# A fixed first expert with its rows gathered turned, two weight pieces loaded earlier, and the gather moved inside an expert block

## The reference, cut to what matters

```
h = layer_norm(ALPHA * x + mix, ln1_g, ln1_b)
logits = h @ router_w + router_b          # top 4 of 32 experts
gates = softmax(top_v)
# tokens sorted by expert into blocks; for each block b with expert e:
gu = xb @ w_gu[e] + b_gu[e]               # 1024 x 2048
act = (clip(up) + 1) * min(gate, 7) * sigmoid(1.702 * min(gate, 7))
out = act @ w_down[e] + b_down[e]         # 1024 x 1024
y = layer_norm(ALPHA * h + sum_k gate_k * out_k, ln2_g, ln2_b)
```

## Time and profile before

| | |
|---|---|
| median of 3 runs | 1522.77 us (1522.66 to 1524.72) |
| profiled execution, its own time | 1524.9 us |
| its span | 1523.1 us |
| PE busy | 1461.6 us (96%) |
| DVE busy | 519.6 us (34%) |
| ACT busy | 263.8 us (17%) |
| POOL busy | 114.1 us (7%) |
| DMA | 507.80 MB, mean 333 GB/s |
| chain that ended last | PE 61%, DMA 25%, DVE 3% |

### The profile page before, as it was taken

How to read it: one execution, slowest core, us unless ns; L and a number is a source line. 1 busy time by engine, 2 the same in 40 slices (tenths; PEclk the granted TensorE clock), 3 DMA queues, 4 the chain that set the end, 5 groups by cost and what they waited for, 6 DMA issues and landing times.

```text
span 1523.1 us, 23088 instructions
## 1 busy us (share of the span) xinstructions
PE 1461.6 (96%) x9245; PEld 743.2 (49%) x9245; DVE 519.6 (34%) x980; ACT 263.8 (17%) x604; POOL 114.1 (7%) x100
## 2 busy tenths in 40 slices
PE   9999999999999998999999999999999999999896
PEld 7777776556777764333333333333333333333332
DVE  3652788767410156122122212211212112122123
ACT  1224214631210014100101001001001001100102
POOL 1002241010503402000000000000000000000000
PEclk9999999999999999999999999999999999999998
DMA  6346687556269648999999999999999999999995
GB/s 211 111 168 179 209 271 232 175 167 195 89 216 331 247 164 316 428 426 429 426 427 428 429 427 429 429 428 428 428 430 428 428 428 429 430 427 428 429 429 205
DMA packets 110621, 507.80 MB, mean 333 GB/s; under 512 B 12600, under 2 KB 49056, under 8 KB 85888
## 3 DMA queue, kind: packets, MB, share of 16 engines
q1 hardware_dynamic: 103884, 499.63, 82.0%
q10 hardware_dynamic: 6676, 7.29, 1.6%
HBM read 491.18 MB, written 15.72 MB: 333 GB/s over the span
## 4 chain that ended last, share of the span: by engine, by line
PE 61%; DMA 25%; DVE 3%; ACT 1%; issue 1%; DVEq 0%; SPq 0%; ACTq 0%
DMA wGU<-in_w_gu 24%; PE ps L2394 12%; PE ps L2399 11%; PE ps L1898 10%; PE ps L2381 5%; PE ps L2202 3%; PE ps L1912 3%; PE ps L2308 2%; PE ps L2216 2%; PE ps L2229 2%; PE ps L2342 2%; PE ps L2316 1%; DMA ringS<-in_ssd_proj 1%; ACT xs L1267 1%; PE ps L2329 1%
## 5 line engine op out<-in xcount | busy, mean ns | idle before, releaser
L2394 PE MATMUL ps<-wGU,xe 128*64 128x512 f32 x1536 | 342.4, 594 | 18.5 <-DMA wGU<-in_w_gu 17.8
L2399 PE MATMUL ps<-wD,aT 128*64 128x512 f32 x1024 | 226.8, 595 | 0.0
L2394 PEld LDWEIGHTS ps<-wGU,xe 128*64 128x64 f32 x1536 | 107.8, 137 | 234.5 <-issue 197.8
L1898 PE MATMUL ps<-xT,ring 128*128 128x288 f32 (+1 forms) x864 | 179.8, 409 | 1.2 <-PEq L200 0.7
L1898 PEld LDWEIGHTS ps<-xT,ring 128*128 128x128 f32 (+1 forms) x864 | 125.1, 170 | 46.0 <-issue 3.5
L2399 PEld LDWEIGHTS ps<-wD,aT 128*64 128x64 f32 x1024 | 70.7, 137 | 131.8 <-issue 127.9
L2381 PE MATMUL ps<-wGU,xe 128*64 128x512 f32 x512 | 121.3, 594 | 11.9 <-DMA wGU<-in_w_gu 11.9
L1791 DVE TENSOR_SCALAR sg<-sg 128x512 f32<-128x512 f32 x32 | 13.7, 427 | 335.4 <-ACT sg L1262 335.4
L1798 DVE COPY ysb<-ps 64x512 f32<-64x512 f32 x32 | 22.2, 694 | 304.8 <-PE ps L2403 304.8
L1262 ACT ACTIVATE sg<-ps 128x512 f32<-128x512 f32 x32 | 19.1, 598 | 471.1 <-PE ps L2386 471.1
L402 PE MATMUL ps<-xT,ring 128*128 128x288 f32 x320 | 78.1, 407 | 0.0
(11 more groups left out here) (476 smaller groups left out, 1445.1 us busy)
## 6 DMA issues: line engine op xcount, KB each, us to landing
wGU<-in_w_gu SPq DMA_DIRECT2D x128, 2048.0 KB, 37.0
wD<-in_w_down SPq DMA_DIRECT2D x64, 2048.0 KB, 37.0
ring<-in_w_in SPq DMA_DIRECT2D x21, 2048.0 KB, 9.2
out<-hst SPq DMA_DIRECT2D x8, 1024.0 KB, 6.0
ringS<-in_ssd_proj SPq DMA_DIRECT2D x4, 2048.0 KB, 10.1
wbuf<-prompt_A_rows ACTq DMA_DIRECT2D x16, 384.0 KB, 4.0
out<-Sb SPq DMA_DIRECT2D x2, 2048.0 KB
ring<-in_hg_proj SPq DMA_DIRECT2D x2, 2048.0 KB, 7.8
```

The lines of the kernel that those rows point to most:

```text
L1898: last = m.matmul(ps[h, b, 0:T], ring[c % 2][:, k, n * P + h.start:n * P + h.stop], xT[:, k, :], start=(k == 0), stop=(k == KD - 1))
L2394: last = m.matmul(ps[half[h], bank, :], xe[:, f, hx, :], wgu[n][:, k, col + CW * h:col + CW * h + CW], start=(i == 0 and k == 0), stop=False)
L2399: last = m.matmul(ps[half[h], B_Y, :], aT[:, k, i - 4, :], wdn[n][:, k, CW * h:CW * h + CW], start=(i == 4 and k == 0), stop=False)
```

## The change

1. Rows are normalised without gamma and beta, by ScalarE in place (`normal`, one activation a tile), and no longer on VectorE. Gamma and beta are applied to the turned rows: `weighed` multiplies and adds per partition from `lnT2`, which two small transposes of `lng4` fill. The copy to `xe` becomes eight small activations a block. ALPHA times gamma and beta (`w5`, `yb`) give the residual (`residual`), which VectorE makes in blocks 0 and 1.
2. The first block is always expert 0: `nb5[:, 0, 0]` is set to 1, and its tokens are found from the counts of expert 0 alone (`first_tokens`). Its rows are gathered turned, in fp32, straight from the rows (`first_rows`), in four quarters, so that `turn_x` and two copies fall away for it. Block 1 is gathered in fp32 from the rows (`gather_rows`). The bf16 parts for the loop are made in block 1 by VectorE and GpSimd (`parts`, t_hp).
3. mT lies in gA and not in gB, so that piece 5 of expert 0 is issued once the branches are merged; piece 3 of expert 1 (buffer 9) is issued after the first half of w_out. If the list is wrong, only expert 1's four pieces are loaded again.
4. In `run` the gather stands ahead of piece 2 (in block 0 ahead of `turn_g`, as before), the bias matmuls stand ahead of piece 3's, and VectorE waits for U by m_f.
5. 8 warming matmuls instead of 12 at the start; the loads of the second LayerNorm's parameters no longer wait for the last gather.

```diff
-                for _ in range(12):
+                for _ in range(8):
...
-        mT = gB
+        mT = gA
...
+                    if n == 0:
+                        sp.wait_ge(t_b3, 1)
+                        piece(1, 3, 9, m_w[9])
                 piece(0, 4, 4, m_w[4])
+                sp.wait_ge(g_m, KD)
+                piece(0, 5, 5, m_w[5])
                 sp.wait_ge(g_mx, 5)
                 piece(1, 0, 6, m_w[6])
                 sp.wait_ge(g_mx, 6)
-                piece(0, 5, 5, m_w[5])
                 piece(1, 1, 7, m_w[7])
                 sp.wait_ge(t_lg, 3)
-                sp.wait_ge(t_h, 5)
+                sp.wait_ge(t_w, 2)
                 piece(1, 2, 8, m_w[8])
-                sp.wait_ge(t_c, 10)
-                piece(1, 3, 9, m_w[9])
...
-                sp.wait_ge(m_x, end + 2)
                 sp.dma_start(lnw2[:], row(ln2_g[0])).then_inc(g_ln, 16)
...
+                def normal(j, t):
+                    rows = TILES[t][1]
+                    act.wait_ge(ln_r, 2 * j + 2)
+                    act.wait_ge(t_ht, (2, 4, 6)[j])
+                    outs = (slice(0, P),) if rows == P else (bands[2], bands[1], bands[0])
+                    for pr in outs:
+                        last = a.activation(xres[pr, t, :], xres[0:rows, t, :], ACT.Identity, scale=var[0:rows, t:t + 1], bias=nmr[0:rows, t:t + 1])
+                    last.then_inc(t_h, 1)
+                def weighed(src, f, h, i):
+                    return a.activation(xe[:, f, h, :], src, ACT.Identity, scale=lnT2[:, f % 2, 2 * h + i:2 * h + i + 1],
+                                        bias=lnT2[:, f % 2, 4 + 2 * h + i:5 + 2 * h + i])
...
+                def first_tokens(t):
+                    rows, (bank, c) = TILES[t][1], ((3, 0), (7, 32), (6, E_))[t]
+                    dstep(v.tensor_tensor(dsel[0:rows, t:t + 1], ps[0:rows, bank, c:c + 1], msk[0:rows, t, 0:1], ALU.mult))
+                    v.tensor_tensor(psel[0:rows, t, :], jcol1[0:rows, :], dsel[0:rows, t:t + 1].broadcast_to([rows, BLK]), ALU.is_equal).then_inc(m_p, 1)
...
+                def first_rows(t, quarters):
+                    rows = TILES[t][1]
+                    for j in quarters:
+                        h, i, bank = QUARTERS[j]
+                        c = CW * h + 256 * i
+                        z = xres[0:rows, t, c:c + 256].rearrange("q (p k) -> q k p", k=2)
+                        for k in range(2):
+                            last = m.matmul(ps[:, bank, BLK * k:BLK * k + BLK], z[:, k, :], psel[0:rows, t, :], start=(t == 2 and k == 0), stop=(t == 1 and k == 1))
+                        if t == 1:
+                            last.then_inc(m_x, 1)
...
+                        if i == gather_at:
+                            pe.wait_ge(m_p, b + 4)
+                            gather()
+                        if i == 3:
+                            pe.wait_ge(m_g, b * 2 + 2)
+                            for bank, col in ((B_G, 0), (B_U, D)):
+                                for h in range(2):
+                                    m.matmul(ps[half[h], bank, :], esel[:], bg3[:, col + CW * h:col + CW * h + CW], start=False, stop=False)
                         if i == 4:
-                            pe.wait_ge(m_p, b + 2)
-                            pe.wait_ge(m_xs, b + 1)
-                            for t in (2, 0, 1):
-                                gather(t)
...
+                                if head and i == 0 and k == 0:
+                                    pe.wait_ge(t_eb, 1)
+                                    m.matmul(ps[0:1, B_S, 0:64], ebc[0:64, 0:1], ident[0:64, 0:64], start=True, stop=True).then_inc(t_tb, 1)
...
+                run(0, 0, 0, None, head=True, gather=gather_rows, gather_at=4)
                 pe.wait_ge(m_ok, 1)
-                run(0, 0, 0, None)
-                run(1, 0, 6, None, (6, 7, 8, 9, 0, 1))
+                run(1, 0, 6, None, (6, 7, 8, 9, 0, 1), gather=gather_rows)
```

More of the change, by code:

```diff
@@ L1228, in _ @@
[L1228 to L1237 removed]
+                turned(3)
+                normal(1, 0)
@@ L1249, in _ @@
[L1249 to L1252 removed]
+                normal(2, 1)
+                act.wait_ge(g_mx, 6)
+                a.activation(yb[:], lnb[:], ACT.Copy, scale=ALPHA).then_inc(t_w, 1)
+                for j, (h, i, bank) in enumerate(QUARTERS):
+                    if j == 0:
+                        continue
+                    act.wait_ge(m_x, j + 1)
+                    for k in range(2):
+                        last = weighed(ps[:, bank, BLK * k:BLK * k + BLK], 2 * i + k, h, i)
+                    last.then_inc(t_xa if j < 3 else m_xc, 1)
@@ L2349, in scatter, with run @@
                         (prompt(j, B_S + j % 3) if j < 4 else samples(B_S + j % 3)).then_inc(m_s, 1)
-                def run(b, turn0, first, pair, places=None):
-                    pe.wait_ge(m_xc, b + 1)
+                def run(b, turn0, first, pair, places=None, head=False, gather=gather_parts, gather_at=2):
+                    if not head:
+                        pe.wait_ge(m_xc, b + 1)
                     for i in range(6):
+                        if head and i < 4:
+                            pe.wait_ge(*((t_x0, 1), (t_xa, 1), (t_xa, 2), (m_xc, 1))[i])
                         n, loaded = (first + i) % RING, turn0 * 64 + 16 * ((first + i) // RING + 1)
```

344 lines of the change are left out of this document (172 added, 172 removed).

## The result

The change makes the kernel slower: 1539.95 us (median of 6 runs, 1535.58 to 1547.54) against 1524.20 for the kernel before beside it (median of 6, 1522.66 to 1529.62). The ratio is 1.0107, with a 95% interval of 1.0083 to 1.0131. The forecast was 1513.9 with a range up to 1520.0, so it was wrong in sign. The experiments ran on several chips; where two of them are compared, the ratio to the kernel before, measured beside each, is the safer number. One execution of all, of a12_g4_pool, took 2172.63 us at a mean granted clock of 0.652, and its ratio leaves that one out.

A forecast was written before the change was run, and what follows sets the result against it. The stream of expert weights was taken as the bound: -8.3 (earlier 11th landing) - 1.1 (tail) + 0.5 (stream pauses) = -8.9 us, off the 1522.77 median, gives 1513.9, range 1510.5 to 1520.

The forecast's parts named there:

- a gap of about 1 us ahead of turn_a in each block: Expert loop: a sign that the forecast is right, TensorE waiting about 1 us before turn_a in every block.
- The pair of blocks: Expert loop: a block without scatter costs 0.86 more, 26.05 us; block pairs take 56.5 us until TensorE meets the stream.
- no DMA waits at all in the last blocks: End of the loop: a sign that the forecast is wrong, meaning TensorE is the bound.
- the first rival: Head: the clock stays at its upper level, so 11.4 us off, 1511.4; chance 0.2.
- The second rival: Loop: TensorE partly becomes the bound, a block costing 1.05 to 1.35 more, 1514 to 1523; chance 0.19.
- the third: Loop: slower, the uncovered activation chain costs over 1.35 more a block; at 1.6 it gives 1530; chance 0.08.
- TensorE has 5.6 us to spare: Whole loop: TensorE's blocks end at 1491.6 against 1497.2 set by the stream, 0.19 us spare a block.
- 8 warming matmuls instead of 12 end 1.7 us earlier: Kernel start: the weights are awaited there anyway, so fewer warming matmuls change the time by 0.
- Eight turning gathers in fp32: Head, behind the last choice: gathers sized by eight router matmuls of like shape, 1.08 us, 0.4 more at low clock.
- The clock: Head: the granted clock falls as before, at half until about 596, so block 0 starts at 591.3.
- Everything that brings this 11th landing forward moves the end one for one: Stream start: the first reload lands at 605.3 instead of 613.6, taking 8.3 us off the end.
- The parts beside each other: Block 1: bf16 parts take near 15 us on GpSimd and about 6 on VectorE, any wait within TensorE's slack.

The follow-up runs named there:

- a12_g4_pool: a12_g4 with the first row tile's three parts made on GpSimd behind its own two tiles instead of on VectorE: 1525.07 us, ratio 1.0011.
- a12_g4_wide: a12_g4_pool with eight more bf16 matmuls of 512 columns between the head's narrow fp32 matmuls: 1527.21 us, ratio 1.0022.
- pool_head: a12_g4_pool with 16 of the 24 fp32 records behind the last choice left out, so block 0 computes wrong rows: 1522.11 us, ratio 0.9988.
- a12_g4: The changed kernel with 12 warming matmuls and the gather ahead of turn_g (piece 4) in every block: 1525.72 us, ratio 1.0008.
- after_gather4: The changed kernel with only the gather moved back ahead of turn_g (piece 4) in every block: 1537.0 us, ratio 1.0098.
- before_8warm: The kernel before with 8 warming matmuls instead of 12 and nothing else: 1528.87 us, ratio 1.0033.
- after_12warm: The changed kernel with 12 warming matmuls again instead of 8: 1530.94 us, ratio 1.0053.
- a12_g4_bias: a12_g4 with the bias matmuls also back behind piece 3's two banks, as in the kernel before: 1526.09 us, ratio 1.0012.
- after_4tiny: The changed kernel with its 8 warming matmuls and four more of a single column behind them: 1535.54 us, ratio 1.0090.
- pool_less: a12_g4_pool with the fp32 gathers of blocks 0 and 1 taking tile 2 alone, 4 records instead of 12: 1524.65 us, ratio 1.0008.

## Why the prediction was wrong, point by point

**Right.** The wait ahead of turn_a, "a gap of about 1 us ahead of turn_a in each block": 1.18. The pair of blocks: 56.45 forecast, 56.68 measured. ScalarE's eight small activations take 2.48 us together inside the 7.09 of the down matmuls, and the LayerNorm loads cost nothing in the tail: 0 each, as forecast. The ways in which it said it would be seen to be wrong, no DMA waits at all in the last blocks and a wait in block 2, are what the profile shows, though that wait stands in the scatter and not ahead of the gather. The clock of the head did fall, so the first rival was out. The second rival had the right mechanism, that TensorE becomes the bound, but tied it to the excess of a block alone (1514 to 1523); the third, slower by the activation chain, needed 1.35 a block, and the chain stayed at 0.97.

**Wrong, in order of size.**

1. "TensorE has 5.6 us to spare". This is the step that failed first: TensorE's blocks ended at 1521.0 and not at 1491.6, and TensorE, not the stream, set the end. This one sum carried the forecast, and every term of it that was small or nothing was taken at its favourable end. The table of 29.4 us shows it: the loop's chain was right, and the rest, added, was five times the spare. The bound between two engines 5.6 us apart over 900 us can't be called by sizing one term well.
2. "8 warming matmuls instead of 12 end 1.7 us earlier ...: 0". It cost 9.0 us here (8.2 by the ratios) and 5.7 in the kernel before. The cover named, the wait for the first weights, exists, but what twelve matmuls also do is to raise the clock ahead of the first real ones, and the program's layout shifts with them (2.4 us of pause). Neither is in a row of the kernel before; a term set to 0 wanted at least a look at the lengths of the matmuls in the first 10 us.
3. The gathers. "Eight turning gathers in fp32 (the eight router matmuls of like shape take 1.08)": the 1.08 stood for eight *records*, and these are four matmuls. In place of 1.08 us on the path stand 5.3 at half clock (24 records), an estimated 2.7 to 3.1 at full clock (half of it, or by the 16 records ahead of the choice in 2.07), and 2.9 in place of 1.3 for the gather of rows, twice.
4. The clock. Taken as low until 596 because it was so before, and it stayed low 10.2 us from a later start. The Trainium skill (TensorE: Matmul & The Clock Gate, What's actually happening) ties the level to how busy the engine was; in the windows above TensorE is booked as busy for 4.20 of 4.20 us right ahead of the fall, and a12_g4_wide did not change it, so the rule alone doesn't forecast this head. The choice was forecast 0.6 earlier; behind the start of mix it comes 42.8 us later instead of 42.95, and 42.7 to 43.8 in the versions with twelve matmuls.
5. "Everything that brings this 11th landing forward moves the end one for one." In the kernel before the reload's issue moved by 1.6 without moving the end. What counts is how long the stream stands still in sum. Where it stands idle for that very release, as in the new head, the release does count: in pool_head it came 2.8 us earlier behind the choice, and the time was 2.3 to 3.0 lower. The forecast had the two early pieces as a gain at the head of the stream, and sized the hole that they leave at 0.5 for pauses; it was 10.2 more than before. With the time from choice to first expert matmul sized right (5.3), the same reasoning gives a first reload near 600.7 and a landing 5.3 us earlier instead of 8.3.
6. The parts beside each other. 10.5 us on VectorE where 6 were forecast, and 19.8 on GpSimd (649.1 to 668.9) where 15 were. The page of the Trainium skill named in the prediction (GPSIMD Engine Reference, 8. Key points) names instructions of VectorE with two SBUF inputs or in a 2-port perf mode, of which the prediction took only the first. Here single-input copies and a cast were longer too, 1.02 and 2.12 against 0.18 for esel; in which mode they ran no run here shows. The price on the path was the scatter's wait of 3.06, and by a12_g4_pool against a12_g4 nothing that can be measured when the stream is the bound.

## What to carry to other kernels

Count an engine's work in the records of the trace, and check the count of one known line against the source before a new line is sized by it: the fp32 matmuls of the router and the gathers had two records each here. When a prefetch is moved into idle time, ask what covered the time that it leaves: a stream that is already unbroken gains only if its next release comes as much earlier as the transfers that were taken out of it. And when two resources end within 1% of each other, a term of nothing has to be measured: four warming matmuls were worth 5.7 and 9.0 us here, and four matmuls a block that fitted into a wait cost 11.3.

## What the runs showed of the hardware that was not expected

TensorE paused 2.4 to 2.6 us in the middle of 128 small matmuls, waiting for nothing recorded, in all three versions with eight warming matmuls (the changed kernel, after_gather4, before_8warm), and in none with four more instructions in front, even of one column. Only in the changed kernel did the clock fall behind it. Matmuls added to the loop brought a like pause of 1.9 to 2.3 us once in six blocks, four times in a run, and behind three of the four, in both versions, the clock was at half for 3.4 us.

The clock fell for 10.2 us in the head although TensorE is booked as busy without a gap in the 3.4 us ahead of it, in the changed kernel and in the profiles of after_12warm, a12_g4_bias and a12_g4_pool. In after_4tiny and pool_less, with the same instructions in the head, it fell for 6.8, so the program alone doesn't set the length. In the kernel before, with real gaps there, the low stretch had 6.8 us in two profiles and 10.2 and another 3.4 in the third, without a later end.

Beside GpSimd's passes over whole rows VectorE's subtraction of 1024 columns took 3.04 us, its cast 1.41 (0.69 in a12_g4, where it began ahead of GpSimd's subtraction) and a copy of 64 columns 1.02 or 2.12, where that copy took 0.18 with GpSimd at rest. GpSimd's own subtraction took 2.45 and its cast 1.92, against 2.13 and 1.04 in a12_g4_pool, where VectorE rested. In a12_g4_pool a small operation of VectorE lasted until the instruction that GpSimd had under way was over: esel from 651.37 to 653.49 beside a subtraction that ended at 653.44, dsel from 654.59 to 655.65 beside a cast that ended at 655.63.
